# Hybrid decoder step: RWKV's eight low-rank steps grouped into the first lot of pages, its other steps from the seventh piece on, and TensorE turning the identity into unused banks in front of five waits

## Chip, cores and metric

One core of one Trainium2 chip runs the whole program. The metric is the device time of one execution in microseconds, as the median of several runs. "PE" is TensorE, "ACT" ScalarE, "DVE" VectorE, "POOL" GpSimd and "SP" SyncE, which only issues transfers here.

## What is computed

The reference is one step of a one-layer decoder. All tokens (512 prompt tokens, 16 meta tokens, 8 sequences with 8 new tokens each) are RMS-normalised and go through one input projection. Half of the projected features feed forgetting attention (8 heads of 64), the other half RWKV-7 time mixing (8 heads of 64). Both results are concatenated and go through an output projection, a SwiGLU FFN and a last RMSNorm. Cut to what matters here:

```python
xn = rms_norm(x, ln1_g);  proj = x_ext @ w_in
# forgetting attention; the new tokens of sequences read 32 pages of 128 past keys and values per sequence
attn = softmax(q k^T / 8 + c_q - c_k) v
# RWKV-7: low-rank steps, then keys' norm, then a recurrence over tokens
w_log = -softplus(-(w0 + tanh(wl) @ w2)) - 0.5;  decay = exp(-exp(w_log))
a = sigmoid(a0 + al @ a2);  g = sigmoid(gl) @ g2
kk = (k * k_k) / max(norm(k * k_k), 1e-12);  k = k * (1 + (a - 1) * k_a)
S = S * decay + (S @ -kk) (kk * a)^T + v k^T;  y = S @ r
out = (group_norm(y) + sum(r * k * r_k) * v) * g
h = x + concat(attn, out) @ w_out;  y = rms_norm(h + ffn(rms_norm(h)))
```

## The kernel before

**Prologue.** For each of five row tiles of x, ACT squares it, DVE scales it (L1902), PE turns it with eight transposes (L741) and DVE copies the turned tile out of PSUM (L1913, `take_rows`). Then eight more transposes (L782) and the input projection follow (L800, 16 instructions for half an item of 301 columns).

**Prompt part.** Projection items, the values' rows (L773) and the prompt's attention in 32 steps share PE until about 324 us.

**Lots.** The past of the eight sequences is read in pairs of sequences, four pages at a time: 4 pairs of 8 lots, 32 lots in all. SP loads each page of keys or values, for both sequences of the pair, into a ring of four slots, and a slot is loaded again once PE has read it. On each engine a generator `all_lots` emits a lot in eight pieces. In a lot `turn_keys` (L1241) turns a page of keys of two sequences in eight transposes, ACT copies it (`take_keys`, L1788, two copies), and `page_scores` (L1255) multiplies it with the queries; `turn_probs` (L1281) turns the previous lot's probabilities, and `lot_values` (L1300) weighs its values. At the end of a lot DVE's `add_scores` (L2288, L2291, L2295) reads the scores, and ACT's `exp_lot` (L1798) exponentiates them in the next lot, ahead of that lot's second pair of key copies. PE turns into two banks in turn, so a second turn after one must wait for the copy of the one before the last.

**RWKV between the pieces.** A second generator `rwkv_rest` holds RWKV's steps, the same number on PE, ACT and DVE. After each piece, every engine runs steps until `rwkv_due(piece)` of them are done; a list `COSTS` gives each step's share. Each engine executes its instructions strictly in the order so written. `rwkv_pre` is the preparation, 17 steps: `row_sums_of` (PE L911), eight `low_rank(j)` (PE L931, two products of 320 columns; ACT's Sigmoid L1661), ACT's Sqrt (L1668) and DVE's reciprocal (L2072) of the key norm, four `spread_norm` (PE L917, DVE L2056), DVE's scans (L2076), and three Exp over 2560 columns (ACT L1683, L1684, L1687). Counted from piece 0, `low_rank(0)` stands behind piece 5, `low_rank(1)` to `(7)` behind pieces 8 to 21, the three Exp behind pieces 24 and 26 (lot 3), and the tiles of the recurrence begin behind piece 46. In the recurrence's last tile, `sample_states`, DVE masks two heads at a time (L2231) and PE multiplies them with keys (L1170), one group g per step; step g=0 stands in piece 5 of lot 23 and step g=1 in its piece 7.

ACT holds one set of function tables; each change of set shows as ACT_TABLE_LOAD. The Sigmoids, the Sqrt and the lots' Exp need three sets. Behind the lots stand the output projection and the FFN, which keep PE full from 905 us to the end.

The lines that set the order are

```python
COSTS = N_PRE * [4] + (12 + 18 * (NTILE - 1)) * [2] + (23 + 16) * [3]
def rwkv_due(piece):
    budget = sum(COSTS) * (piece + 1) // (8 * LOTS - 20)
    return sum(c <= budget for c in itertools.accumulate(COSTS))
rest, done = rwkv_rest(), 0
for piece, _ in enumerate(all_lots()):
    while done < rwkv_due(piece):
        next(rest)
        done += 1
```

## Time and profile before

| | |
|---|---|
| median of 3 runs | 1407.38 us (1405.04 to 1408.07) |
| profiled execution, its time | 1404.47 us |
| profiled execution, its span | 1402.7 us |
| PE busy | 1309.2 us, 93% of the span |
| DVE, ACT, POOL busy | 567.0, 387.1, 110.6 us |
| mean granted clock of PE | 0.985 |
| HBM traffic | 203.06 MB read, 14.41 MB written |

The span leaves out 1.8 us of the execution's time. The profiled execution lies 2.9 us under the median. The page says where engines are busy; a list by stretch shows busy time, granted clock (1.00 is 2.4 GHz, 0.50 is 1.2 GHz) and the DMA engines' share; the list of waits names who released an idle engine; the timeline gives single instructions.

### The profile page before, as it was taken

How to read it: one execution, taken by the hardware profiler on the slowest of the kernel's cores; microseconds unless marked ns; L12 is line 12 of the kernel's file. 1: busy time of each engine (PE TensorE's matmuls, PEld its weight loads, DVE VectorE, ACT ScalarE, POOL GpSimd, SP SyncE). 2: the span in 40 equal slices, each digit the busy share in tenths (PEclk: the TensorE clock that was granted, in tenths of full speed). 3: DMA queues.
4: the chain of work that ended last, by engine and by line, in shares of the span. 5: the costliest groups of instructions: out<-in, count | busy, mean ns of one | idle time of the engine just before them, and what ended most of it. 6: DMA issues, size and time to landing. Idle time of an engine off the chain costs nothing.

```text
span 1402.7 us, 28552 instructions
## 1 busy us (share of the span) xinstructions
PE 1309.2 (93%) x11707; PEld 953.8 (68%) x11707; DVE 567.0 (40%) x1084; ACT 387.1 (28%) x769; POOL 110.6 (8%) x219
## 2 busy tenths in 40 slices
PE   5999999997889999999998789999999999999997
PEld 4764666665567677777774555457777777778886
DVE  5012355554573443443426233255334333372322
ACT  3010333235654444435452453210000000000001
POOL 6273200000000000000300101000000000000000
PEclk9999999998999999999999999999999999999999
DMA  6167310006688777778886988901123113123101
GB/s 221 61 140 181 111 61 10 29 0 229 231 308 300 231 230 268 228 255 273 255 275 203 366 309 285 306 7 60 61 61 119 61 60 101 42 83 124 42 8 61
DMA packets 128844, 219.37 MB, mean 156 GB/s; under 512 B 11484, under 2 KB 46375, under 8 KB 128711
## 3 DMA queue, kind: packets, MB, share of 16 engines
q1 hardware_dynamic: 120818, 193.64, 41.4%
q0 software_dynamic: 7824, 23.85, 6.2%
q8 instruction: 93, 1.52, 0.5%
q14 instruction: 41, 0.33, 0.1%
q10 hardware_dynamic: 68, 0.02, 0.0%
HBM read 203.06 MB, written 14.41 MB: 155 GB/s over the span
## 4 chain that ended last, share of the span: by engine, by line
PE 86%; DVE 6%; ACT 3%; issue 2%; DMA 2%; SPq 0%; POOL 0%; POOLq 0%; DVEq 0%; ACTq 0%
PE PS L1435 21%; PE PS L800 13%; PE PS L1517 9%; PE PS L1241 7%; PE PS L1255 4%; PE PS L1367 4%; PE PS L1300 4%; PE PS L773 2%; DMA out_wkv_prompt<-arena 1%; PE PS L1526 1%; PE PS L1055 1%; PE PS L1059 1%; PE PS L1065 1%; PE PS L882 1%; PE PS L1281 1%
## 5 line engine op out<-in xcount | busy, mean ns | idle before, releaser
L1435 PE MATMUL PS<-arena 128*128 128x288 f32 x1232 | 300.3, 405 | 1.1 <-issue 0.6
L1435 PEld LDWEIGHTS PS<-arena 128*128 128x128 f32 x1232 | 232.2, 189 | 68.1 <-DVE arena L2525 1.0
L800 PE MATMUL PS<-arena 128*128 128x301 f32 (+1 forms) x736 | 195.9, 423 | 0.0
L1788 ACT ACTIVATE arena<-PS 128x512 f32<-128x512 f32 x256 | 140.9, 595 | 166.7 <-PE PS L1241 166.7
L800 PEld LDWEIGHTS PS<-arena 128*128 128x128 f32 (+1 forms) x736 | 135.5, 187 | 53.9 <-issue 12.3
L1241 PE MATMUL PS<-arena 128*128 128x128 f32 x1024 | 145.5, 283 | 20.1 <-ACT arena L1788 7.1
L1241 PEld LDWEIGHTS PS<-arena 128*128 128x128 f32 x1024 | 115.2, 144 | 47.9 <-issue 25.9
L1517 PE MATMUL PS<-arena 128*128 128x256 f32 x616 | 134.4, 379 | 0.0
L1517 PEld LDWEIGHTS PS<-arena 128*128 128x128 f32 x616 | 116.2, 189 | 17.7 <-issue 0.8
L1255 PE MATMUL PS<-arena 128*32 128x128 f32 x2048 | 83.6, 280 | 0.1
L1300 PE MATMUL PS<-arena 128*32 128x256 f32 x1024 | 68.7, 385 | 2.6 <-DMA arena<-in_cache_v 1.9
L1255 PEld LDWEIGHTS PS<-arena 128*32 128x32 f32 x2048 | 51.0, 110 | 24.0 <-issue 17.3
L1367 PE MATMUL PS<-arena 128*128 128x512 f32 x128 | 59.1, 602 | 0.0
L2140 DVE TENSOR_TENSOR arena<-PS,arena 128x512 f32<-128x512 f32 (+2 forms) x56 | 36.0, 660 | 48.6 <-PE PS L1055 35.9
L2325 DVE SCALAR_TENSOR_TENSOR arena<-arena,PS 128x256 f32<-128x256 f32 x32 | 15.4, 480 | 82.3 <-PE PS L1300 82.1
L2578 DVE TENSOR_TENSOR arena<-PS,arena 128x256 f32<-128x256 f32 x36 | 14.4, 422 | 80.9 <-PE PS L1517 80.9
L1300 PEld LDWEIGHTS PS<-arena 128*32 128x32 f32 x1024 | 28.3, 109 | 27.7 <-issue 12.5
L1599 ACT ACTIVATE arena<-PS 128x602 f32<-128x602 f32 (+1 forms) x23 | 15.5, 673 | 105.3 <-PE PS L800 105.3
L1367 PEld LDWEIGHTS PS<-arena 128*128 128x128 f32 x128 | 22.8, 189 | 26.5 <-issue 26.5
L651 POOL DMA_DIRECT2D forgets_after<-arena x64 | 36.9, 601 | 47.3 <-DVE arena L1958 32.8
L2508 DVE TENSOR_TENSOR arena<-PS,arena 128x288 f32<-128x288 f32 x22 | 10.1, 458 | 73.5 <-PE PS L1435 73.5
L414 POOL DMA_DIRECT2D out_y_sample<-arena x2 | 1.1, 537 | 483.4 <-DVE arena L2621 483.4
(383 smaller groups left out, 1510.4 us busy)
## 6 DMA issues: line engine op xcount, KB each, us to landing
arena<-in_cache_k SPq DMA_DIRECT2D x256, 256.0 KB, 4.2
arena<-in_cache_v SPq DMA_DIRECT2D x256, 256.0 KB, 4.4
arena<-in_w_gate SPq DMA_DIRECT2D x11, 1024.0 KB, 5.5
arena<-in_w_up SPq DMA_DIRECT2D x11, 1024.0 KB, 8.1
arena<-in_w_down SPq DMA_DIRECT2D x8, 1408.0 KB, 6.4
arena<-in_w_in SPq DMA_DIRECT2D x5, 2048.0 KB, 11.7
forgets_after<-arena POOLq DMA_DIRECT2D x64, 128.0 KB, 8.5
arena<-forgets_after SPq DMA_DIRECT2D x32, 256.0 KB, 5.1
```

The lines of the kernel that those rows point to most:

```text
L651: pool.dma_start(forgets_after[b, DS * h:DS * h + DS].rearrange("t (c k) -> c t k", k=PAGE), src)\
L773: ins = mm(o, xnT[:, k, 17 + P * (i - 1):17 + P * i], w, start=(k == 0), stop=(k == KT - 1))
L800: ins = mm(PS[0:width, bank, 0:HALF], wring[:, c % 2, k, c0:c0 + width], xnT[:, k, half * HALF:(half + 1) * HALF], start=(k == 0), stop=(k ...
L1241: ins = tr(PS[:, bank, g * P:(g + 1) * P], Kr[:, i, q, g * P:(g + 1) * P], ident)
L1255: ins = mm(PS[ROWS[2 * q + gp], SCORE, i * P:(i + 1) * P], QB[:, 2 * (L // NLOT) + q, g, :], KTs[:, (2 * i + q) % LOT, g, :], start=(gg == ...
L1300: ins = mm(PS[ROWS[r], OUT, 0:QW], PTs[:, i, ROWS[r]], Vr[:, i, r // 2, QW * (r % 2):QW * (r % 2) + QW], start=(i == 0), stop=(i == LOT - ...
L1367: ins = mm(PS[rows, E + 2 * (n % 2) + half, :], mixT[:, k, cols], wo[:, k, half * NB:(half + 1) * NB], start=(k == 0), stop=(k == KT - 1), ...
L1435: ins = mm(PS[:, bank, 0:HO], weights[:, j], moving[:, j], start=(first and j == 0), stop=(j == KH - 1), skip_group_check=not first)
L1517: ins = mm(PS[:, bank, 0:QC], weights[:, j, q * P:(q + 1) * P], moving[:, j], start=(first and j == 0), stop=(j == NR - 1), skip_group_che ...
L1599: av(dst.rearrange("p (a b) -> p a b", a=2), src, ACT.Copy, scale=scale).then_inc(S["proj_taken"], 1)
L1788: av(KTs[:, (2 * i + q) % LOT], PS[:, T_USE[("k", L, i, q)] % 2, :].rearrange("p (g n) -> p g n", g=NG), ACT.Copy)\
L2140: return tt(dst, src, mask.unsqueeze(1).unsqueeze(1).to_broadcast([n_p, a, b, n]), ALU.mult)
```

## The change

`keep_busy(n, bank)` lets PE turn the identity n times into a bank that nothing reads. It is called in six lines, around five waits or rows of waits: 24 turns before the parameters are waited for; 16, 8, 7 and 9 after the turns of row tiles 1 to 4; 12 on either side of `new_scores(0)`; 30 ahead of the first group of `sample_states`; 12 ahead of the spread of the last norm. They are 130 turns in all.

The first step of `rwkv_rest` (now `row_sums_of` and `low_rank(0)`) runs before the first piece, and the other low-rank steps stand behind pieces 0, 1 and 2: two, two and three of them. In the last of these ACT also takes the gate's Sigmoid, which stood before the lots, and the Sqrt. Nothing more of RWKV runs until piece 9; from there the steps follow at nearly the old rate. `spread_norm` gets four steps of its own, the three Exp are cut into halves, one half per step, and DVE's scans move to the second piece's step, ahead of the reciprocal. The tiles of the recurrence come in the same piece or one piece earlier than before. The new tokens' Exp (`exp_new(0)`) moves from before the lots to piece 3, its turn and copy to piece 6.

```diff
         SMP = NTILE
-        N_PRE = 17
+        N_PRE = 18
 
...
         HALVES = [slice(0, 64), slice(64, P)]
-        COSTS = N_PRE * [4] + (12 + 18 * (NTILE - 1)) * [2] + (23 + 16) * [3]
+        N_AHEAD = 4
+        COSTS = N_AHEAD * [0] + (N_PRE - N_AHEAD) * [4] + (12 + 18 * (NTILE - 1)) * [2] + (23 + 16) * [3]
         N_RWKV = len(COSTS)
...
                 if L % NLOT == 0:
-                    if i == 2 and L < LOTS:
+                    if i == (2 if L else 3) and L < LOTS:
                         use_t(("n", L // NLOT), "prn_taken", L // NLOT + 1)
...
         def rwkv_due(piece):
-            budget = sum(COSTS) * (piece + 1) // (8 * LOTS - 20)
+            if piece + 2 < N_AHEAD:
+                return piece + 2
+            budget = sum(COSTS) * max(0, piece - 6) // (8 * LOTS - 27)
             return sum(c <= budget for c in itertools.accumulate(COSTS))
...
+
+            def keep_busy(n, bank):
+                for _ in range(n):
+                    tr(PS[:, bank, 0:P], ident, ident)
+
+            keep_busy(24, 6)
             pe.wait_ge(S["par_in"], 16 * (len(PAR_ROWS) + 2))
...
                 ins.then_inc(S["xT_turned"], 1)
+                keep_busy((0, 16, 8, 7, 9)[i], 6)
             pe.wait_ge(S["xnT_ready"], NTILE)
...
                 pe.wait_ge(S["consts"], 4)
-                pe.wait_ge(S["lr_act"], 2)
-                g, bank = j % 4, E + 2 * (j % 2 if j < 4 else 1)
+                pe.wait_ge(S["lr_act"], 1)
+                g, bank = j % 4, E + 2 * (j % 2)
                 if j == 1:
                     pe.wait_ge(S["root_in"], 1)
                 elif j:
-                    pe.wait_ge(S["lr_taken"], j - 1 if j < 4 else j)
+                    pe.wait_ge(S["lr_taken"], j - 1)
                 w = slice(g * P, (g + 1) * P)
...
                 if n == 0:
-                    pe.wait_ge(S["lr_taken"], 3)
+                    pe.wait_ge(S["lr_taken"], 7)
                 else:
...
             def rwkv_pre():
-                yield
+                low_rank(0)
                 row_sums_of(T2, 1, E + 2)
-                low_rank(0)
                 yield
...
                 low_rank(3)
-                spread_norm(0)
-                yield
-                for n in range(3):
-                    low_rank(4 + n)
-                    spread_norm(n + 1)
-                    yield
+                low_rank(4)
+                yield
+                low_rank(5)
+                low_rank(6)
                 low_rank(7)
                 yield
-                for _ in range(6):
+                for n in range(NG):
+                    spread_norm(n)
+                    yield
+                for _ in range(7):
                     yield
...
                 yield
+                keep_busy(30, E + 2)
                 for g in range(NG):
...
                 pe.wait_ge(S["g2_in"], 16)
+                pe.wait_ge(S["lr_act"], 2)
                 for g in range(NG):
...
                 yield
+                keep_busy(12, E + 2)
                 pe.wait_ge(S["hs_in"], 6)
...
                         lot_values(L - 1, 0)
-                    if j == 0:
+                    if j == 0 and L:
                         turn_new(pr)
...
                         lot_values(L - 1, 1)
+                    else:
+                        turn_new(0)
                     yield
...
             ins.then_inc(S["rn_turned"], 1)
+            keep_busy(12, OUT)
             new_scores(0)
+            keep_busy(12, OUT)
             def rows_of(i):
...
 
-            rest, done = rwkv_rest(), 0
+            rest, done = rwkv_rest(), 1
+            next(rest)
             for piece, _ in enumerate(all_lots()):
...
             av(XR[0:64, 12, :], XR[0:64, 12, :], ACT.Tanh).then_inc(S["lr_act"], 1)
-            av(XR[:, 13, :], XR[:, 13, :], ACT.Sigmoid).then_inc(S["lr_act"], 1)
-
...
                 act.wait_ge(S["lr_ready"], j + 1)
-                bank = E + 2 * (j % 2 if j < 4 else 1)
+                bank = E + 2 * (j % 2)
                 src = PS[:, bank:bank + 2, 0:TL // 2]
...
             def rwkv_pre():
-                yield
                 low_rank(0)
                 yield
+                low_rank(1)
+                low_rank(2)
+                yield
+                low_rank(3)
+                low_rank(4)
+                yield
+                low_rank(5)
+                low_rank(6)
+                low_rank(7)
+                av(XR[:, 13, :], XR[:, 13, :], ACT.Sigmoid).then_inc(S["lr_act"], 1)
                 act.wait_ge(S["root_in"], 1)
                 av(Rn, Rn, ACT.Sqrt).then_inc(S["root_done"], 1)
-                low_rank(1)
-                low_rank(2)
-                yield
-                low_rank(3)
-                yield
-                low_rank(4)
-                yield
-                low_rank(5)
-                yield
-                low_rank(6)
-                yield
-                low_rank(7)
+                yield
                 yield
                 act.wait_ge(S["L_ready"], 1)
-                av(AR[:, 1], Kd, ACT.Exp, scale=-E_HALF).then_inc(S["decays"], 1)
-                av(AR[:, 0], AR[:, 0], ACT.Exp, scale=-E_HALF).then_inc(S["decays"], 1)
-                yield
-                act.wait_ge(S["decays"], 1)
-                av(Kd, Kd, ACT.Exp, scale=E_HALF).then_inc(S["decays"], 1)
-                yield
+                for n, (dst, src, scale) in enumerate(((AR[:, 1], Kd, -E_HALF), (AR[:, 0], AR[:, 0], -E_HALF), (Kd, Kd, E_HALF))):
+                    if n == 2:
+                        act.wait_ge(S["decays"], 2)
+                    for half in (slice(0, 2), slice(2, 4)):
+                        av(dst[:, half], src[:, half], ACT.Exp, scale=scale).then_inc(S["decays"], 1)
+                        yield
                 for _ in range(7):
...
                     take_keys(L, 2)
+                    if L == 0:
+                        exp_new(0)
                     yield
...
             av(RNT, PS[:, SCORE, :].rearrange("p (r n) -> p r n", r=NPAIR)[:, :, 64:P], ACT.Copy).then_inc(S["rn_taken"], 1)
-            exp_new(0)
-            rest, done = rwkv_rest(), 0
+            rest, done = rwkv_rest(), 1
+            next(rest)
             for piece, _ in enumerate(all_lots()):
...
                 yield
+                for g in range(NG):
+                    dve.wait_ge(S["lr_taken"], g + 1)
+                    ch(v.tensor_tensor_scan(Kd[:, g], chunk_mask, AR[:, 0, g], 0.0, ALU.mult, ALU.add))
+                yield
                 dve.wait_ge(S["root_done"], 1)
                 v.reciprocal(Rn, Rn).then_inc(S["hs_in"], 1)
                 yield
-                dve.wait_ge(S["lr_taken"], 4)
-                for g in range(NG):
-                    ch(v.tensor_tensor_scan(Kd[:, g], chunk_mask, AR[:, 0, g], 0.0, ALU.mult, ALU.add))
                 norm_keys(0)
-                yield
-                norm_keys(1)
                 ch.wait()
                 tt(AR[:, 0], Kd, AR[:, 0], ALU.subtract).then_inc(S["L_ready"], 1)
                 yield
-                norm_keys(2)
-                yield
-                norm_keys(3)
-                yield
+                for n in range(1, NG):
+                    norm_keys(n)
+                    yield
                 dve.wait_ge(S["hs_taken"], 4)
...
                 yield
-                dve.wait_ge(S["decays"], 3)
                 ch(tt(Bd, Bd, kk, ALU.mult))
                 yield
+                dve.wait_ge(S["decays"], 4)
                 ch(stt(AR[:, 0], kk, -1.0, AR[:, 0], ALU.mult, ALU.mult))
...
                 ch.wait()
+                dve.wait_ge(S["decays"], 6)
                 ch(tt(Bd, Bd, Kd, ALU.mult))
...
                     yield
-                    if j == 0:
+                    if j == 0 and L:
                         take_new_probs(pr)
                     yield
                     yield
+                    if L == 0:
+                        take_new_probs(0)
                     if L:
...
 
+            rest, done = rwkv_rest(), 1
+            next(rest)
             dve.wait_ge(S["rn_taken"], 1)
             add_new(0)
-            rest, done = rwkv_rest(), 0
             for piece, _ in enumerate(all_lots()):
```

## Rows read from the trace of the kernel before

**Rows 1.** The page, part 1: engines' busy time over the whole span.

```profile
PE 1309.2 (93%) x11707; PEld 953.8 (68%) x11707; DVE 567.0 (40%) x1084; ACT 387.1 (28%) x769; POOL 110.6 (8%) x219
```

**Rows 2.** Lots 1, 3, 4: length; PE, PEld, DVE, ACT, POOL; clock; DMA share, GB/s.

```profile
343.00:368.00 25.00, 19.91 (x170) 14.07 (x171) 15.94 (x15) 15.90 (x23) 0.00 (x0) 0.86 0.69 236
382.50:397.80 15.30, 9.46 (x124) 6.76 (x122) 11.10 (x13) 12.38 (x13) 0.00 (x0) 0.78 0.68 232
397.80:408.60 10.80, 9.15 (x135) 6.46 (x136) 10.66 (x14) 5.65 (x11) 0.00 (x0) 1.00 1.01 360
```

**Rows 3.** By stretch, PE alone: the stretches at the lower clock.

```profile
271.40:278.20 6.80, 6.26 (x18) 0.50 0.01 2
326.00:336.20 10.20, 6.30 (x52) 0.50 0.95 319
349.90:356.70 6.80, 4.43 (x11) 0.50 0.28 103
387.40:394.30 6.90, 4.64 (x40) 0.51 0.34 118
749.20:756.10 6.90, 6.05 (x19) 0.51 0.01 4
```

**Rows 4.** Timeline of the prologue; in brackets idle time and releaser.

```profile
8.73 0.33 PE L735 MATMUL PS<-arena 58*128 58x58 f32 x1 [8.73 <-DMA ptab<-in_page_table]
...
16.42 1.97 PE L741 MATMUL PS<-arena 128*128 128x128 f32 x8 [2.39 <-DVE arena L1902]
...
22.31 1.27 DVE L1913 TENSOR_TENSOR arena<-PS,arena 128x512 f32<-128x512 f32 x2
22.44 1.97 PE L741 MATMUL PS<-arena 128*128 128x128 f32 x8 [1.03 <-DVE arena L1902]
24.45 1.29 DVE L1913 TENSOR_TENSOR arena<-PS,arena 128x512 f32<-128x512 f32 x2 [0.87 <-PE PS L741]
25.79 1.88 PE L782 MATMUL PS<-arena 128*9 128x128 f32 x8 [1.38 <-DVE arena L1913]
27.47 2.72 PE L800 MATMUL PS<-arena 128*128 128x301 f32 x7
```

**Rows 5.** Timeline, PE, start of the lots.

```profile
326.85 0.66 PE L1268 MATMUL PS<-arena 128*32 128x64 f32 x16 [2.29 <-ACT arena L1829]
330.53 3.97 PE L1241 MATMUL PS<-arena 128*128 128x128 f32 x16 [3.02 <-DMA arena<-in_cache_k]
341.75 0.65 PE L1255 MATMUL PS<-arena 128*32 128x128 f32 x16
```

**Rows 6.** Waits of PE from 323.9 to 410 us: total, times, longest.

```profile
PE PS L1281 <- ACT arena L1788: 11.5, 3, 5.8
```

**Rows 7.** Groups of ACT by line, 323.5 to 392 us: busy us, mean ns.

```profile
L1661 ACT ACTIVATE arena<-PS,arena 128x640 f32<-128x640 f32 x8 | 6.2, 794 | 4.1 <-PE PS L931 4.1
L1661 ACT ACT_TABLE_LOAD x4 | 5.1, 1283 | 0.1
L1683 ACT ACTIVATE arena<-arena 128x2560 f32<-128x2560 f32 x1 | 2.3, 2337 | 0.0
```

**Rows 8.** Groups of DVE by line, 323.5 to 424 us.

```profile
L2072 DVE RECIPROCAL arena<-arena 128x640 f32<-128x640 f32 x1 | 4.2, 4153 | 2.4 <-ACT arena L1668 2.4
```

**Rows 9.** Chain that ended last: start, us; eight key turns, two low-rank products.

```profile
365.62 1.03 PE PS L1241 x8
366.64 1.10 PE PS L931 x4
```

**Rows 10.** Timeline around `sample_states`, PE, then DVE.

```profile
740.77 1.93 PE L1170 MATMUL PS<-arena 64*64 64x512 f32 x8
750.05 3.67 PE L1170 MATMUL PS<-arena 64*64 64x512 f32 x8 [4.66 <-DVE arena L2231]
...
747.50 2.50 DVE L2231 TENSOR_TENSOR arena<-arena 64x512 f32<-64x512 f32 x4
```

**Rows 11.** Timeline, PE, the last norm's spread.

```profile
828.65 1.35 PE L917 MATMUL PS<-arena 128*128 128x320 f32 x4 [1.97 <-DVE arena L2265]
```

More of the change, by code:

```diff
@@ L1663, in rwkv_pre @@
             def rwkv_pre():
-                yield
                 low_rank(0)
                 yield
-                act.wait_ge(S["root_in"], 1)
-                av(Rn, Rn, ACT.Sqrt).then_inc(S["root_done"], 1)
                 low_rank(1)
```

2 lines of the change are left out of this document (added).

## Prediction

> **What bounds the kernel.** I began with the page's busy times: PE is busy 1309.2 us of a span of 1402.7, everything else under half of it [rows 1]. So a change pays only if it removes idle time of PE, time at the lower clock, or work, and here 130 turns are added. Next I listed busy time and granted clock by stretch. Each stretch at the lower clock follows idle time on PE, and in it the same work takes twice as long: 16 key turns took 3.97 us at 330.5 us, and 8 took 1.03 us at 365.6 us [rows 5, 9]. The five stretches in the lots, the attention and the recurrence cost half their busy time: 3.1, 3.2, 2.2, 2.3 and 3.0 us [rows 3]. The records show no clock for the first 29 us, but 8 turns take 1.97 us there, which is the lower clock's time [rows 4]. Then I went through the first lots, which the change rewrites. Lot 1 takes 25.0 us, of which PE is busy 19.9; lot 3 takes 15.3 with 9.5 busy; lot 4 takes 10.8 with 9.15 busy and a DMA share of 1.01 [rows 2]. So in lots 1 and 3 PE waits for somebody, and in lot 4 the transfers are the limit. The list of waits names one: L1281, `turn_probs`, waited three times, 11.5 us in all, the longest 5.8 [rows 6]. Its releaser is written as the key copies, but these stand in ACT's order behind table loads, low-rank Sigmoids and, in lot 3, two whole Exp of 2.3 us each: it is ACT's order that PE waits for.
>
> **Prologue.** 24 turns at the lower clock are 24 x 1.97/8 = 5.9 us; PE sat idle there until 8.7 us [rows 4], so they cost nothing and may raise the clock. The turns after row tiles 1 to 4 lie in idle time of 1.0 to 2.4 us a tile [rows 4]: at full clock (1.03/8 = 0.13 us [rows 9]) 16 take 2.1 us and 7 to 9 take 0.9 to 1.2 us. DVE sets the pace of the tiles, so nothing is won before the last. Behind it, if the clock is full: DVE's last copy starts at 23.6 (end of the one before) and not at 24.45, which is 0.85 us; L782 takes 1.0 and not 1.88 us; and the first seven of L800 take about 1.9 and not 2.72 us [rows 4]. The sum is 2.5 us, and it goes through whole, since PE has no idle time in the next 100 us. With gaps left between the bursts the clock may fall again before the last tile, and then 16 turns at the lower clock (3.9 us in a gap of 2.4) delay the chain a little. I take -2.0, with bounds +1.5 and -2.6.
>
> **Start of the lots.** Before, PE waited 2.29 us for ACT and 3.02 us for the first keys [rows 5]. The keys land at 330.5 whatever PE does. Up to then PE now has 12 turns (1.6 us), the new scores (0.5), 12 turns (1.6), `low_rank(0)` (1.1) and the row sums (1.3), from 324.6: it ends with the row sums near 330.4, since these wait for DVE's squares until 328.9. So the 24 turns cost nothing. They hold the clock, and the stretch from 326.0 to 336.2 no longer costs its 3.2 us (part of which was hidden under arriving keys: I count 2.5).
>
> **Low-rank steps in lot 0.** A low-rank step is two products, four instructions, and 1.10 us at full clock [rows 9], and ACT takes 0.8 us for each [rows 7], so PE and ACT alternate without a stall. From 330.5 PE has seven steps (7.7 us), three pages of keys (3.3) and two page scores (1.3): it is through at 342.7. ACT then still has the last Sigmoid (0.8), the gate's Sigmoid (0.8), a table load (1.3 [rows 7]), the Sqrt (0.8), and only then the copies of the third page. The fourth page's turn needs the bank of the third: PE waits from 342.7 to about 345. Another table load and `exp_new(0)` (1.8 us) stand ahead of the fourth page's copies, which holds PE another 1.3 and 0.5 us. DVE's reciprocal (4.2 us [rows 8]) follows the Sqrt and ends at 348.6, just as `new_values` would ask for the copy queued behind it. Lot 0 so ends near 349.5, 6.5 us later than before, with 7.7 us of low-rank work done ahead. These waits add up to 4.3 us, and busy time is so thin from 342.7 to 348 that I expect the clock to fall once: +2.5 us, as the other falls cost.
>
> **Lots 1 to 4.** Before, ACT loaded tables ten times from the gate's Sigmoid to the first long Exp, four of them ahead of low-rank Sigmoids at 1.28 us each [rows 7]; now three loads do, and the seven saved are 9.0 us of ACT's time. The waits of L1281 go, 11.5 us, and two stretches of lower clock with them, 2.2 and 2.3 us. The halved Exp put 1.2 us in front of a copy where 4.7 or more stood. Then the limit of lot 4 takes over. A lot moves 16 pages of 128 x 512 floats and a bias of the same size, 4.46 MB. At the 360 GB/s of a full DMA that is 12.4 us, while lot 4 took 10.8, since its first pages lay in the rings already [rows 2]. I take 11.8, between the two. PE alone needs 9.15 us [rows 2]. So my walk is: lot 0 ends at 349.5; lot 1 has three spreads, 9.2 + 3 x 1.2 + 1 for small waits = 13.7, and 2.5 for the clock: 365.7; three lots at 11.8: 401.1. Before, the same point, with the same RWKV steps done but for one pair of sums, stood at 408.6. I take -7.5. Without the transfers' limit lots 2 to 4 would take 3 x 9.6 = 28.8 us, which is 6.6 better; with new waits as long as a whole Exp on DVE's side (its steps are 2.8 us each, and three a lot and the lots' own work nearly fill DVE) it could be -2. These are the bounds: -2 and -14.
>
> **Thirty turns before the first group of new states.** They stand ahead of the step g=0. There PE arrived at 740.7 and waited 0.3 us; the long wait of 4.66 us is that of g=1 [rows 10]. Behind g=0 PE weighs values and scores pages, DVE adds the scores, ACT exponentiates, DVE takes the new scores, and only then comes the masking (2.50 us at 747.5) that g=1 waits for. That whole chain hangs on PE's work after the 30 turns, so it moves by them: 30 x 0.13 = 3.9, less 0.3. The wait of 4.66 us stays, and the fall of the clock in it too. +3.5; bounds 0 (if the chain had slack that I don't see) and +4.1.
>
> **The rest.** Twelve turns (1.6 us) before the last norm's spread lie in a wait of 1.97 us [rows 11]: 0. From piece 45 on the steps come in the same piece or one earlier, so order and waits are those of before: 0.
>
> **Sum.** -2.0 - 7.5 + 3.5 = -6.0 us against the profiled execution, 1404.5, gives 1398.5. That execution is 2.9 us under the median; -6.0 from 1407.4 gives 1401.4. I forecast **1401**.
>
> **Does turning hold the clock?** The trace says so: at the lower clock from 326.0, PE was idle or turned keys for most of the time (16 turns from 330.5 on, 3.97 us), and at 336.2 the clock rose [rows 3, 5]. By that the turns count as work. The Trainium skill (TensorE: Matmul & The Clock Gate, Part 4: PE-mode transpose) says the contrary, that transposes don't count as busy in the same way and full clock doesn't engage for them; by it the sum would lose the clock terms, and the time would be that of the third rival below. The trace disagrees with it here.
>
> **Rivals.** (1) *The transfers don't bind and the clock holds.* For it: DMA had a share of only 0.68 and 0.69 in lots 1 and 3 [rows 2], so the rings might be full when the fast lots come, and a lot took 10.8 us, not 11.8. Three lots at 10.8 are 3 us better, no fall in lot 0 another 2.5, the prologue 0.5: -12, 1395.5. Chance 0.20. (2) *Given back.* The waits in lot 0 grow (ACT's copies of page 3 behind Sqrt, DVE's reciprocal ahead of the new tokens' probabilities), the clock falls twice, and lots 2 to 4 run at the transfers' pace anyway: lots -3, prologue -1, thirty turns +3.5: 1407, no change. Chance 0.15. (3) *Turns don't hold the clock*, the one that ends slower. Then the turns after tiles 1 to 4 take 3.9, 2.0, 1.7 and 2.2 us at 0.246 each, longer than the gaps, and by following the tiles L800 starts 4.2 us late; the 24 around the new scores take 5.9 us and make the first key turn 3.3 us late; the lots' waits still go but their clock terms don't: -7.5 + 3.3 + 2.5; the thirty cost 3.5. With the prologue's 4.2 instead of -2.0 the sum is +6.0: 1413. It decides from the point where a burst of turns ends after its wait does, some 10 turns a gap. Against it stands the rise at 336.2. Chance 0.08. The forecast itself has 0.57.
>
> **Range and chances.** What a measurement of this kernel can tell from no change is 0.2%, 2.8 us: faster means under 1404.6, slower over 1410.2. The forecast's own range is 1396 to 1406, the clock's falls alone being worth 2 to 3 us each and not tied to the program where they come by chance. With the first two rivals inside I give 1394 to 1408. Faster: 0.50 of the first case, all of rival 1, a little of rival 2: 0.72. Slower: rival 3 and the edge of rival 2: 0.09. Same: 0.19.
>
> **What the profile after would show.** L782 at 1.0 us and L800 starting near 25.9: the prologue's step is right; turns of 0.25 us there: wrong. `add_scores` of lots 0 and 4 near 347 and 399 (both 2 us earlier than in the walk, for the prologue): right; lots 2 to 4 with a DMA share near 1.0 show the transfers as the limit. L1281's waits on ACT under 3 us in all; one lower-clock stretch between 320 and 400 and not three. A wait of about 4.7 us before L1170's second group and none filled before the first: the thirty turns are cost. If the wait before g=1 has shrunk instead, that step is wrong. The forecast fails most easily if lots 2 to 4 are faster than 11.8 us or if a new wait of DVE's stands before `exp_lot`.

## The result and the profile after

The changed kernel takes **1388.64 us** (median of 4 runs, 1388.36 to 1392.19) against 1406.41 for the kernel before, a ratio of 0.9875 with a 95% interval of 0.9856 to 0.9894: 17.8 us faster. Forecast were 1401 and a range of 1394 to 1408. The direction was right and the size was a third of what came; the time lies below the range.

The page of the changed kernel, part 1, answers to [rows 1]:

```profile
span 1386.2 us, 28803 instructions
PE 1315.2 (95%) x11837; PEld 962.3 (69%) x11837; DVE 566.6 (41%) x1084; ACT 376.4 (27%) x765; POOL 111.0 (8%) x219
```

PE does 130 instructions more and is busy 6.0 us more, and the span is 16.5 us shorter: idle time went. ACT lost 10.7 us of work, which is mostly table loads.

The stretches of the changed kernel between the `add_scores` of lots 0 to 4, as in [rows 2] (PE, PEld, DVE, ACT, POOL; clock; DMA share, GB/s):

```profile
344.30:356.40 12.10, 11.51 (x149) 8.10 (x142) 7.00 (x11) 7.96 (x13) 0.00 (x0) 1.00 0.95 330
356.40:367.90 11.50, 10.91 (x141) 7.87 (x142) 5.75 (x13) 9.01 (x14) 0.00 (x0) 1.00 0.96 328
367.90:378.90 11.00, 9.44 (x138) 6.97 (x139) 10.86 (x14) 6.71 (x13) 0.00 (x0) 1.00 1.03 376
378.90:389.60 10.70, 8.93 (x130) 6.07 (x129) 10.56 (x13) 5.64 (x11) 0.00 (x0) 1.00 1.05 386
```

Lots 1 to 4 took 66.1 us together and now take 45.4. The DMA share is 0.95 or more in each, where it was 0.69 and 0.68 in lots 1 and 3. It doesn't follow that the transfers set the length of a lot. In lots 1 and 2 PE is busy all but 0.6 us. In lots 3 and 4 it is DVE: busy 10.86 of 11.0 and 10.56 of 10.7 us, and in its timeline nothing stands idle from one `add_scores` (L2302) to the next. The last operations of lot 3:

```profile
375.73 2.82 DVE L2113 TENSOR_TENSOR arena<-arena 128x2560 f32<-128x2560 f32 x1
378.47 0.48 DVE L2339 SCALAR_TENSOR_TENSOR arena<-arena,PS 128x256 f32<-128x256 f32 x1
378.86 0.69 DVE L2302 TENSOR_TENSOR arena<-PS,arena 128x512 f32<-128x512 f32 x1
```

PE ends the page scores at 378.04, 0.8 us before DVE comes to them. The chain of work that ended last names, from 367.9 to 395.0 us, DVE alone and "issue", time in which an engine waits for nothing that the profile shows; no transfer and no other engine stands in it. Its longest pieces on DVE there:

```profile
369.43 2.82 DVE arena L2106
373.35 2.47 DVE arena L2110 x3
375.82 1.89 DVE arena L2113
380.38 2.82 DVE arena L2116
386.50 2.22 DVE arena L2125
391.14 2.82 DVE arena L2128
```

The kernel before had the same limit in its lot 4: DVE is busy 10.66 of 10.8 us there [rows 2], and from 397.8 us to the next `add_scores` at 408.6 its chain too names DVE and "issue" alone. The waits of PE in the changed kernel from 345 to 395 us, where [rows 6] had 11.5 us on one line:

```profile
PE PS L1254 <- ACT arena L1806: 1.6, 4, 0.9
PE PS L1254 <- ACT arena L1801: 1.4, 4, 0.3
PE PS L1254 <- DMA arena<-in_cache_k: 0.7, 2, 0.6
PE PS L1313 <- DMA arena<-in_cache_v: 0.6, 1, 0.6
PE PS L1294 <- ACT arena L1801: 0.4, 1, 0.4
```

The turn of probabilities (now L1294) waits 0.4 us. The prologue of the changed kernel on PE, which answers to [rows 4] (L740 are the turns of the identity, L750 those of the row tiles, L792 and L810 what follows):

```profile
2.75 4.32 PE L740 MATMUL PS<-arena 128*128 128x128 f32 x24 [2.75 <-POOL arena L577]
...
13.67 3.09 PE L740 MATMUL PS<-arena 128*128 128x128 f32 x16
16.60 1.04 PE L750 MATMUL PS<-arena 128*128 128x128 f32 x8
...
24.86 1.05 PE L792 MATMUL PS<-arena 128*9 128x128 f32 x8 [0.40 <-DVE arena L1928]
25.75 1.94 PE L810 MATMUL PS<-arena 128*128 128x301 f32 x7
```

L792 takes 1.05 instead of 1.88 us, L810 starts at 25.75 instead of 27.47, and its first seven take 1.94 instead of 2.72. The first group of new states, answering to [rows 10], PE and then DVE:

```profile
718.53 3.50 PE L740 MATMUL PS<-arena 128*128 128x128 f32 x30
721.95 1.94 PE L1181 MATMUL PS<-arena 64*64 64x512 f32 x8
731.24 3.68 PE L1181 MATMUL PS<-arena 64*64 64x512 f32 x8 [4.66 <-DVE arena L2245]
...
728.67 2.51 DVE L2245 TENSOR_TENSOR arena<-arena 64x512 f32<-64x512 f32 x4
```

The thirty turns stand in front of the first group, and the second group's wait is 4.66 us, to the hundredth what it was.

All kernels were then laid beside each other by the same marks: the start of the first projection item, the turn of the new tokens' mask that opens the lots, and the `add_scores` of lots 0, 4, 22 and 24. Executions differ by a few us, in part by where the clock falls, so the parts say more than the totals. (us; the last column is the length of the stretch at the lower clock near 270 us, in the prompt's attention.)

| kernel | first item | mask turned | to lot 0 | lots 1-4 | lots 5-22 | 23-24 | near 270 |
|---|---|---|---|---|---|---|---|
| before | 27.5 | 323.9 | 18.6 | 66.1 | 317.7 | 43.7 | 6.8 |
| changed | 25.8 | 318.5 | 25.8 | 45.4 | 314.5 | 48.0 | none |
| changed, again | 25.1 | 320.9 | 25.9 | 46.7 | 314.9 | 47.6 | 6.8 |
| order only | 27.3 | 324.1 | 26.7 | 45.8 | 319.8 | 43.7 | 6.8 |
| turns only | 24.8 | 319.2 | 18.3 | 66.1 | 319.1 | 47.9 | 3.4 |
| no thirty | 24.7 | 317.4 | 26.1 | 45.4 | 317.0 | 44.9 | none |
| thirty later | 25.1 | 317.7 | 25.9 | 45.4 | 316.7 | 41.4 | none |
| no prologue turns | 26.7 | 322.1 | 25.8 | 45.6 | 318.7 | 47.2 | 3.4 |
| the same, again | 26.4 | 323.1 | 25.8 | 46.7 | 318.2 | 47.6 | 6.8 |
| no scores turns | 24.6 | 317.3 | 25.4 | 45.9 | 317.7 | 47.9 | none |
| lots loaded | 25.9 | 321.6 | 25.9 | 48.7 | 319.6 | 47.5 | 6.8 |
| whole Exp | 25.9 | 318.6 | 25.7 | 48.0 | 319.1 | 47.9 | none |
| halves in before | 27.4 | 323.9 | 18.8 | 65.3 | 318.0 | 43.7 | 6.8 |
| tables back | 24.9 | 319.3 | 26.5 | 53.7 | 315.4 | 47.0 | 3.4 |
| best1 | 25.9 | 320.2 | 25.7 | 45.6 | 315.7 | 41.4 | 3.4 |
| no start 24 | 25.8 | 318.5 | 25.6 | 45.4 | 318.2 | 47.7 | none |
| no tile turns | 27.4 | 323.1 | 25.6 | 45.4 | 315.9 | 47.2 | 3.4 |
| best2 | 25.8 | 320.1 | 25.7 | 45.5 | 315.9 | 41.4 | 3.4 |

By these marks the 16.5 us of the profiled executions are: up to the mask -5.5, lot 0 +7.2 (the low-rank steps done there), lots 1 to 4 -20.7, lots 5 to 22 -3.2, lots 23 and 24 +4.3, behind them +1.4.

### The profile page after: what moved, and what is told of

The parts are those of the page before. It is cut to its first block, busy times and chain, and to the rows that moved or that the text cites. A ratio compares the mean times of both kernels' runs of the same rounds, so it can differ in the third digit from the quotient of the medians.

```text
span 1386.2 us, 28803 instructions
## 1 busy us (share of the span) xinstructions
PE 1315.2 (95%) x11837; PEld 962.3 (69%) x11837; DVE 566.6 (41%) x1084; ACT 376.4 (27%) x765; POOL 111.0 (8%) x219
## 4 chain that ended last, share of the span: by engine, by line
PE 86%; DVE 6%; ACT 3%; issue 2%; DMA 2%; SPq 0%; POOL 0%; POOLq 0%; DVEq 0%; ACTq 0%
PE PS L1453 22%; PE PS L810 13%; PE PS L1535 9%; PE PS L1254 7%; PE PS L1268 4%; PE PS L1384 4%; PE PS L1313 4%; PE PS L783 2%; DMA out_wkv_prompt<-arena 1%; PE PS L1544 1%; PE PS L1075 1%; PE PS L1065 1%; PE PS L1069 1%; PE PS L892 1%; PE PS L927 1%
## 5 line engine op out<-in xcount | busy, mean ns | idle before, releaser
L810 PE MATMUL PS<-arena 128*128 128x301 f32 (+1 forms) x736 | 193.0, 418 | 0.0
L810 PEld LDWEIGHTS PS<-arena 128*128 128x128 f32 (+1 forms) x736 | 133.6, 185 | 52.6 <-issue 10.2
L2154 DVE TENSOR_TENSOR arena<-PS,arena 128x512 f32<-128x512 f32 (+2 forms) x56 | 35.9, 658 | 47.2 <-PE PS L1065 32.8
L1313 PEld LDWEIGHTS PS<-arena 128*32 128x32 f32 x1024 | 28.0, 108 | 26.9 <-issue 10.8
L1384 PEld LDWEIGHTS PS<-arena 128*128 128x128 f32 x128 | 22.8, 189 | 26.5 <-issue 26.5
## 6 DMA issues: line engine op xcount, KB each, us to landing
arena<-in_w_in SPq DMA_DIRECT2D x5, 2048.0 KB, 11.7
```

Source lines behind the costliest of these rows:

```text
L810: ins = mm(PS[0:width, bank, 0:HALF], wring[:, c % 2, k, c0:c0 + width], xnT[:, k, half * HALF:(half + 1) * HALF], start=(k == 0), stop=(k ...
L1313: ins = mm(PS[ROWS[r], OUT, 0:QW], PTs[:, i, ROWS[r]], Vr[:, i, r // 2, QW * (r % 2):QW * (r % 2) + QW], start=(i == 0), stop=(i == LOT - ...
L1384: ins = mm(PS[rows, E + 2 * (n % 2) + half, :], mixT[:, k, cols], wo[:, k, half * NB:(half + 1) * NB], start=(k == 0), stop=(k == KT - 1), ...
L2154: return tt(dst, src, mask.unsqueeze(1).unsqueeze(1).to_broadcast([n_p, a, b, n]), ALU.mult)
```

## Experiments

**The order without the turns, and the turns without the order.** `order_only` takes all six calls of `keep_busy` out of the changed kernel; `turns_only` puts them into the kernel before.

```diff
-            keep_busy(24, 6)
...
-                keep_busy((0, 16, 8, 7, 9)[i], 6)
...
-                keep_busy(30, E + 2)
...
-                keep_busy(12, E + 2)
...
-            keep_busy(12, OUT)
             new_scores(0)
-            keep_busy(12, OUT)
```

> The changed kernel without any of the 130 turns of the identity; the order of the steps is the new one. Theory (the order gives most of the gain, by freeing ACT in lots 0 to 3; the turns give only the clock at two places and cost the thirty): against the changed kernel it loses 2.5 us in the prologue and 2.5 to 3 us of lower clock behind 330 us, and wins 3.3 us by the missing thirty: 1389 to 1392. Lots 0 to 4 take what they take in the changed kernel within 3 us. Rival (the turns hold the clock all through lots 0 to 4 and this is most of the gain): 1396 or more, with two or three stretches of lower clock between 320 and 400 us.

> The kernel before with the same 130 turns at the same places, steps in the old order. Theory (order gives most): prologue -2.5, the stretch of lower clock after 326 us gone, -2.5, the thirty turns +3.3: 1404 to 1406, and the wait of 5.8 us before the turn of probabilities in lot 3 is still there. Rival (the turns are the gain): under 1398.

Measured: order only 1394.18 us (ratio 0.9914, 0.9895 to 0.9933), turns only 1405.07 (0.9994, 0.9977 to 1.001). The time of the first is 2 us above what the theory gave and under the rival's, though two stretches of lower clock came, as the rival had it (3.4 us each, from 329.7 and 346.8); that of the second is the theory's. From the mask's turn to the scores of lot 4 the order alone takes 72.5 us and the changed kernel 71.2, where the kernel before takes 84.7 and the turns alone leave 84.4. So the whole gain of the lots is the order's. Up to the mask it is the other way: the turns alone gain and the order can't.

**The thirty turns.** `no_thirty` takes them out, `thirty_later` has them ahead of the second group, in that group's own bank:

```diff
-                keep_busy(30, E + 2)
                 for g in range(NG):
+                    if g == 1:
+                        keep_busy(30, E + 3)
                     pe.wait_ge(S["um_ready"], 2 * g + 2)
```

> The changed kernel without the thirty turns ahead of the first group of new states. Theory of the prediction (they delay the chain that the second group's wait hangs on, at full price less 0.3 us): 3.3 to 3.6 us faster than the changed kernel, 1385.2, the wait of 4.7 us before the second group unchanged. Rival (they hold the clock or lie in a wait): the same time within 1 us, or slower, with a longer stretch of lower clock behind them.

> The changed kernel with the thirty turns ahead of the second group instead of the first, into that group's own bank. Theory: the wait of 4.7 us becomes 0.8 us of wait and 3.9 us of turns, the chain isn't delayed, and the clock doesn't fall behind it, which cost about 3 us: 1382 to 1383.5, 5 to 6.5 us faster than the changed kernel. Rival (the fall of the clock there has another cause): the time of the kernel without the thirty.

Measured: 1386.32 us (ratio 0.9858, 0.9840 to 0.9876) without, 1384.62 (0.9845, 0.9829 to 0.9861) later. In lots 23 and 24 the four kernels stand at 48.0 (first group), 44.9 and 43.7 (none; two kernels) and 41.4 us (second group). Ahead of the first group the turns cost 3.1 to 4.3 us, moved one step they win 2.3 to 3.5. The two kernels with none differ in the clock too: it fell for 10.2 us in `no_thirty` and for 6.8 in `order_only`. The timeline of PE in `thirty_later`:

```profile
724.79 3.50 PE L740 MATMUL PS<-arena 128*128 128x128 f32 x30
729.52 1.93 PE L1182 MATMUL PS<-arena 64*64 64x512 f32 x8 [1.23 <-DVE arena L2246]
```

The wait is 1.23 us of what was 4.66, and the second group takes 1.93 instead of 3.68 us, since the clock no longer fell. The theory gave 5 to 6.5 us; the totals give 4.0 and, against the second measurement of the changed kernel, 6.8, and the part gives 6.6.

**The prologue's turns.** `no_prologue_turns` and `no_prologue_again` are one kernel, without the 24 and without those after the tiles; `no_start_24` and `no_tile_turns` lack one of the two calls each.

> The changed kernel without the 24 turns at the start and those after the row tiles; all others stay. Theory (the prologue's turns bring the full clock to its last row tile, and nothing later depends on them): the first projection item starts 1.7 to 2.8 us later and its first instructions run at the lower clock; 3 us slower than the changed kernel in all, 1391.6. Rival (they also keep the clock in the prompt's attention 270 us in, where the kernel before and the one without any turns each show a stretch at the lower clock and three of four kernels with them show none): that stretch comes back, 3 us more, 1394 to 1395.

> The kernel without the prologue's turns once more. By the profiles the turns are worth 3.0 us up to the turn of the mask, once the stretches of lower clock near 270 us are taken out; its median was 6 to 9 us above the changed kernel's two. Theory (3 us and chance): 1391 to 1395. Rival (they are worth 6 us or more by something later): 1396 to 1398 again.

> The changed kernel without the 24 turns at the start, with those after the row tiles. Theory (the 16 turns after the second tile raise the clock by themselves, since in the changed kernel it had fallen again by then): the first projection item starts as early as with them, within 0.5 us; the time of the changed kernel. Rival (a cold start of the 16 delays the tiles, or the clock rises too late): 1 to 3 us slower.

> The changed kernel with the 24 turns at the start and none after the row tiles. Theory (the clock falls in the tiles' gaps, and the last tile is turned at the lower clock): as slow as the kernel without both, the first item starting 1.7 to 2.8 us later. Rival (the 24 turns are enough): the time of the changed kernel.

Measured: 1397.62 and 1398.32 us without both (ratios 0.9950 and 0.9949, 0.9932 to 0.9969 and 0.9932 to 0.9966), 1393.74 without the 24 (0.9891 to 0.9937), 1394.81 without the tiles' (0.9901 to 0.9935). Which call counts shows in the timelines of PE. First `no_tile_turns`:

```profile
22.37 1.97 PE L750 MATMUL PS<-arena 128*128 128x128 f32 x8 [1.03 <-DVE arena L1916]
25.72 1.88 PE L791 MATMUL PS<-arena 128*9 128x128 f32 x8 [1.38 <-DVE arena L1927]
```

Then `no_start_24`:

```profile
24.92 1.05 PE L791 MATMUL PS<-arena 128*9 128x128 f32 x8 [0.40 <-DVE arena L1927]
```

Without the tiles' turns the last tile and L791 run at the lower clock as in the kernel before; without the 24 nothing is lost up to the first item, to 0.1 us. So the 24 do nothing there: the clock they raise falls again before the row tiles. The tile turns bring the first item 1.7 us forward and shorten its first seven instructions by 0.8: 2.5 us. Up to the mask it is 2.5 to 3 us: the six kernels with them and without a fall near 270 us stand at 317.3 to 318.6, and the four without them and with a fall of 6.8 us at 323.1 to 324.1, of which 3.1 us is the fall's. The medians lie further off: 6 to 10 us from the changed kernel's two without both calls, 3 to 6 without the tiles' turns, and 2 to 5 without the 24. Some of this is the fall near 270: it came in all six profiled executions without the tile turns and in six of twelve with them. The rest of the distance isn't explained by any stretch that the profiles show, and stays open.

**The turns around the new scores.**

> The changed kernel without the 12 and 12 turns around the new tokens' first scores. Theory (with the new order PE has low-rank work before the first keys, so the clock is nearly safe there; without any turns the stretch from the turn of the new tokens' mask to the scores of lot 4 took 72.5 us and with them 71.2 to 71.5): 1 to 1.5 us slower, 1389.5 to 1390. Rival (they are what saves the clock at the start of the lots): a stretch of 6.8 us or more at the lower clock there and 3 us lost, 1391.5 or more.

Measured: 1390.88 us (0.9890, 0.9872 to 0.9909), between the theory's and the rival's. The parts say nothing is lost: 25.4 us to lot 0 and 45.9 in lots 1 to 4, and no fall at 326. The order gives PE low-rank work while it waits for the first keys, and that is enough for the clock here and in `best2` below. It wasn't in `order_only`, where these turns are missing too: there the clock fell for 3.4 us at 329.7, and lot 0 ended 26.7 us after the mask. What the 24 turns save is nothing in two executions and may be up to 1 us in the third.

**What limits lots 2 to 4.** `lots_loaded` gives PE eight turns more in six steps that are empty on PE:

```diff
-                for _ in range(7):
+                for n in range(7):
+                    if n < 6:
+                        pe.wait_ge(S["lr_taken"], 8)
+                        keep_busy(8, E + 2)
                     yield
```

> The changed kernel with eight more turns of the identity, 1.03 us of PE, in each of six steps of lots 2 to 4 in which PE has nothing of RWKV to do. Theory A (transfers limit lots 2 to 4, as the prediction had it): lots 2 to 4 keep their 11.5, 11.0 and 10.8 us within 0.5 us each, and the time stays within 1.5 us of the changed kernel's. Theory B (PE and its waits for ACT limit them, the rings' reserve covers the transfers): the 6.2 us show in full, 1394.5 to 1395. In between: the share that shows is PE's.

Measured: 1395.65 us (0.9934, 0.9916 to 0.9952). From the scores of lot 1 to those of lot 4 it takes 35.4 us against 33.3, to those of lot 5 52.0 against 49.5. The stretches of `lots_loaded` for lots 2 to 4:

```profile
360.80:373.20 12.40, 11.81 (x149) 8.78 (x150) 5.77 (x13) 9.01 (x14) 0.00 (x0) 1.00 1.00 352
373.20:385.20 12.00, 11.40 (x158) 9.12 (x159) 11.03 (x14) 6.66 (x12) 0.00 (x0) 1.00 1.03 362
385.20:396.20 11.00, 10.41 (x149) 8.12 (x149) 10.72 (x13) 5.54 (x11) 0.00 (x0) 1.00 1.03 374
```

Of 6.2 us added, 2.1 to 2.5 show. Lot 2 has one of the six bursts and gets longer by 0.9 us, all of it: PE is the limit there. Lot 3 has three, 3.3 us, and gets longer by 1.0. Lot 4 has two, 2.2 us, and gets longer by 0.2 to 0.3. So in lots 3 and 4 something else than PE sets the pace, but theory A has the wrong name for it. DVE stays busy 11.03 us in lot 3 and 10.72 of the 11.0 in lot 4; in lot 3 it now waits 0.83 us for PE, in lot 4 for nobody. PE's waits for transfers, 1.3 us in these two lots of the changed kernel, are gone here, and lot 4 isn't shorter for it. No run lightened DVE, so this limit is read from the traces and not from an experiment on DVE alone. The total is 4 to 7 us higher than the changed kernel's two. The profiled execution, the slowest of six, has falls of the clock near 270, 344 and 535 us; the changed kernel's second execution has the first two of them, its first none of this length. What the median's distance consists of isn't shown.

**Whole Exp in the changed kernel, halves in the kernel before.**

```diff
-                    for half in (slice(0, 2), slice(2, 4)):
-                        av(dst[:, half], src[:, half], ACT.Exp, scale=scale).then_inc(S["decays"], 1)
-                        yield
+                av(AR[:, 1], Kd, ACT.Exp, scale=-E_HALF).then_inc(S["decays"], 1)
+                av(AR[:, 0], AR[:, 0], ACT.Exp, scale=-E_HALF).then_inc(S["decays"], 1)
+                yield
```

> The changed kernel with the three Exp whole, as before: two of 2.3 us in one step, the third in the next, and no halves. Theory (whole Exp stand in ACT's order ahead of the key copies and were the wait of 5.8 us in lot 3): PE waits 3 to 5 us once between the scores of lots 0 and 3, and the clock may fall behind it, 2 us: 3 to 6 us slower, 1392 to 1395. Rival (the moved low-rank steps, not the halves, made the gain; ACT has time in lots 1 to 3 now that no tables are loaded): less than 1.5 us.

> The kernel before with nothing changed but the three long Exp of 2560 columns: the first two cut into halves that stand one to a step, the third into halves that stand together in the next step. Theory (whole Exp in ACT's order were the wait of 5.8 us of the turn of probabilities in lot 3, and the clock fell behind it): that wait shrinks to under 2 us, the lower clock near 387 us goes, 4 to 7 us faster than before. Rival (the wait goes to another place, because a table load and DVE's long operations stand there too): under 2 us faster.

Measured: whole Exp 1395.27 us (0.9929, 0.9909 to 0.9950), of which 2.6 us lie in lots 1 to 4; a wait of PE of this size appears in lot 1:

```profile
PE PS L1268 <- ACT arena L1801: 2.4, 1, 2.4
```

Halves in the kernel before: 1403.59 us (0.9976, 0.9961 to 0.9992), but only 0.8 us of it in lots 1 to 4. Lot 3 took 11.6 instead of 15.3 us, and lot 4 13.7 instead of 10.8: the waits of `halves_in_before` from 343 to 424 us show a turn of probabilities still waiting, five times and 10.2 us in all, 4.7 of them in lot 1, where low-rank Sigmoids and table loads are where they were.

```profile
PE PS L1281 <- ACT arena L1789: 10.2, 5, 4.7
```

Lot 4 has no low-rank step. What it lost it lost on DVE, which waited 2.85 us for halves of the third Exp (L1687) and was busy all the rest of the lot:

```profile
397.17 2.83 DVE L2104 SCALAR_TENSOR_TENSOR arena<-arena 128x2560 f32<-128x2560 f32 x1 [1.23 <-ACT arena L1687]
402.15 2.83 DVE L2111 TENSOR_TENSOR arena<-arena 128x2560 f32<-128x2560 f32 x1 [1.62 <-ACT arena L1687]
```

So the halves are worth 2.6 us in the new order and almost nothing in the old. The theory was right about the wait of lot 3; the rival was right that the time goes to another place, DVE's long operations in lot 4.

**Table loads put back.** `tables_back` has a Sigmoid of one column ahead of the second half of each Exp:

```diff
                     for half in (slice(0, 2), slice(2, 4)):
+                        if half.start:
+                            av(small[:, 4:5], small[:, 4:5], ACT.Sigmoid)
```

> The changed kernel with a Sigmoid of one column, on data that nobody reads, ahead of the second half of each of the three Exp, so that ACT loads two tables (2.56 us) in each of three steps of lots 1 to 3. Theory (table loads in ACT's order among the lots were the other half of what PE waited for): 3 to 6 us slower than the changed kernel from the turn of the mask to the scores of lot 4. Rival (ACT has room in these lots, and the transfers set the pace anyway): under 1 us there.

Measured: 1398.83 us (0.9944, 0.9923 to 0.9966). Lots 1 to 4 take 53.7 us instead of 45.4 and 46.7. The groups of ACT in `tables_back` from 345 to 395 us:

```profile
L1701 ACT ACT_TABLE_LOAD x3 | 3.8, 1283 | 0.1
L1702 ACT ACT_TABLE_LOAD x3 | 3.8, 1283 | 0.0
```

7.7 us of table loads on an engine that is busy 7.3 of 11.3 us a lot cost 7.0 to 8.3 us, more than the theory gave. They don't cost it evenly: lot 1 is as long as before (12.1 us), lot 2 is 3.1 us longer, lot 3 5.2 and lot 4 not at all. Two stretches of lower clock came with them (3.4 and 6.8 us from 372.6 and 379.5, PE busy 3.40 and 5.18 us in them); at half clock that is up to 4.3 us of the sum, nearly all in lot 3. So the waits behind the loads and the clock that fell in them have about equal parts. This is the experiment that says what the old order cost.

**Two better versions.** `best1` is `thirty_later` with 14 turns in lot 0's wait for the Sqrt; `best2` is `thirty_later` without the 36 turns around the new scores and before the last norm's spread.

```diff
+                    if L == 0:
+                        pe.wait_ge(S["lr_taken"], 7)
+                        keep_busy(14, E)
                     turn_keys(L, 3)
```

> The changed kernel with the thirty turns ahead of the second group of new states (as in the kernel that had them there) and 14 more turns in lot 0, ahead of the fourth key page's turn, where PE waited 2.7 us for ACT behind the Sqrt and the clock fell for 3.4 us. Theory: against the kernel with the thirty moved alone 1 to 1.7 us from the start of the lots to the scores of lot 1, no lower clock near 340 us; 1383. Rival (the turns only move the fall by a few us, since ACT's next table load leaves another gap): no difference.

> The changed kernel with the thirty turns ahead of the second group and without the 12 and 12 around the new scores and the 12 before the last norm's spread. Theory (these 36 lie in waits and hold nothing that counts): the time of the kernel that has them, 1384.4 within 1.5 us. Rival (they save a fall of the clock each, 1.5 to 3 us): 1386 or more.

Measured: 1384.22 us (0.9837, 0.9816 to 0.9858) and **1383.14 us** (0.9844, 0.9824 to 0.9864). They and `thirty_later` can't be told apart. In `best1` the fall near 340 us is gone, lot 0 ends 25.7 us after the mask instead of 25.9, and lots 1 to 4 take the same 45.6 us: a clock that falls for 3.4 us there costs nothing. In its place stands a wait of 1.08 us for key copies that ACT has behind a table load and `exp_new(0)`:

```profile
344.74 0.41 PE L1289 MATMUL PS<-arena 128*64 128x128 f32 x2 [1.08 <-ACT arena L1805]
```

A fall of 6.8 us, in the changed kernel's second execution, cost 1.3 us of lot 1. The 36 turns of `best2` do nothing that shows in its time.

**The changed kernel again.**

> The changed kernel once more, unaltered, beside the others of this batch: how far its 1388.6 us, its absent stretch of lower clock in the prompt's attention and its short lots 5 to 22 (314.5 us between two scores where seven other kernels took 316.7 to 319.8) were chance. Theory (they were lucky): 1389 to 1392, with lots 5 to 22 at 316 to 320 us. Rival (they belong to the kernel): 1388.5 within 1 us and 314 to 315 us again.

Measured: 1391.44 us (0.9877, 0.9855 to 0.9900), so the ratio to the kernel before is what it was, and the total is the theory's; lots 5 to 22 are the rival's. The fall near 270 us came, and the mask is turned 2.4 us later; lots 5 to 22 took 314.9 us again. The three kernels with the old order took 317.7 to 319.1 us there, the fifteen with the new one 314.5 to 319.8; the five with a fall of the clock in it stand at 318.2 or more, the ten without at 314.5 to 318.2. If anything of the gain lies there it is 1 to 2 us.

## Why the prediction was wrong

**Reading of the bound: right for lots 1 and 3, wrong for lot 4.** PE's idle time behind ACT in lots 1 and 3 was the place of the gain, and `tables_back` confirms that table loads among the lots are paid in full, waits and clock together. In lot 4 the prediction named the transfers, by their share of 1.01; the limit was DVE's order, busy 10.66 of 10.8 us in the same row. And the chain of the kernel before goes in lot 1 not only through three table loads but also through DVE's scans (L2076, 5.64 us from 356.4), which the change moved as well; no run moves them alone, so their part of the gain in lot 1 stays open.

**Lots 1 to 4, -7.5: the step that failed.** "Then the limit of lot 4 takes over" was priced as the transfers' pace, 11.8 us a lot, and lot 1 at 16.2 us. From the mask to lot 4 the change gave -13.5 us (-12.1 in the second execution). The removals that the prediction listed come to 16 us (11.5 of waits, 4.5 of clock) and the new waits in lot 0 to 4.3; the difference, 11.7, was close. The walk then took back more than was due. It let lot 0 end 25.6 us after the mask, and it took 25.8. It gave lot 1 13.7 us with three spreads and 2.5 for a fall of the clock: the third spread stands behind lot 1's scores, the fall came in lot 0 and lasted 3.4 us, and lot 1 took 12.1 (13.4 where a fall of 6.8 us reached into it). And it gave lots 2 to 4 11.8 us each as the transfers' pace, 35.4; they took 33.3. That makes 4.1 and 2.1 us of the 6.0, with 0.2 the other way in lot 0. The second term is wrong in its mechanism and not only in its size: lot 2's 11.5 us are PE's, and the 11.0 and 10.8 us of lots 3 and 4 are DVE's order, back to back. DMA moved 376 and 386 GB/s in these two lots, above the 360 from which I had worked out 12.4 us, and the slots still held enough that PE waited for transfers only 1.3 us in both together, none of it on the chain. That 11.8 came within 1 us of each lot is luck.

**Lot 0: right.** PE was to wait from 342.7 to 345 behind the gate's Sigmoid and the Sqrt. In the changed kernel, 5.5 us earlier:

```profile
335.77 1.04 PE L1254 MATMUL PS<-arena 128*128 128x128 f32 x8
340.07 1.70 PE L1254 MATMUL PS<-arena 128*128 128x128 f32 x8 [2.68 <-ACT arena L1801]
```

A wait of 2.68 us, and the clock fell once behind it, for 3.4 us. `best1` showed that the fall cost nothing; I had counted 2.5 us.

**Prologue, -2.0: right, and 0.5 us short.** The first item started 1.7 us earlier and its first seven instructions took 0.8 us less, 2.5 us, which is the sum that the prediction worked out before it took 2.0; up to the mask the kernels give 2.5 to 3 us. The 24 turns that I let "may raise the clock" did raise it, and it fell again before the first tile; the tile turns did the work.

**What was not in the sum.** A fall near 270 us cost the profiled execution of before 3.1 us, which the changed kernel's profiled execution didn't have. The prediction named such falls as chance and left them out of the sum. It came in twelve of the eighteen profiled executions, more often without the tile turns; the cause isn't settled. Lots 5 to 22, for which the prediction had 0, took 3.2 us less in the profiled execution; 1 to 2 of them may be the change's.

**The start of the lots: right in time, the reason only in part.** The clock held there, but `no_scores_turns` and `best2` show that it holds without the 24 turns too; in `order_only` it fell for 3.4 us instead of 10.2.

**Thirty turns, +3.5: right.** 3.1 to 4.3 us were measured, the wait of 4.66 us stayed where it was, and the clock fell in it. That it fell for 10.2 us instead of 6.8 isn't the turns' doing: in `no_thirty` it was 10.2 as well. **The last norm's twelve, 0: right**; the row behind them, answering to [rows 11], waits 0.51 us instead of 1.97:

```profile
810.15 1.53 PE L740 MATMUL PS<-arena 128*128 128x128 f32 x12
812.19 1.35 PE L927 MATMUL PS<-arena 128*128 128x320 f32 x4 [0.51 <-DVE arena L2279]
```

**Does turning hold the clock?** Yes. In the changed kernel the low stretch ended at 16.1 us, after 28 instructions that are all turns, 16 of tiles and 12 of the identity (length, busy us of PE, clock, DMA share, GB/s):

```profile
9.25:16.10 6.85, 5.90 (x28) 0.50 0.98 319
16.10:25.70 9.60, 7.18 (x62) 1.00 1.04 394
```

The second stretch too has only turns in it, 62 of them, and stays at full clock. The rule of the Trainium skill (TensorE: Matmul & The Clock Gate, Part 4: PE-mode transpose), that full clock doesn't engage for transposes, doesn't hold here: 1.00 was granted through those 62.

**The rivals.** The first (-12, 1395.5) was nearest, and still 7 us short. Its premise, that the transfers don't bind, is what the traces show for lots 1 to 4; but it took 10.8 us for lot 2 as well, which PE holds at 11.5, and it kept the high price of lot 1, 13.7 us. The second, that the waits in lot 0 give the gain back, is closed by the 71.2 us from the mask to lot 4 against 84.7. The third needed turns that don't raise the clock.

**The range: too narrow below.** The lots' own bound was -14 and the runs came to -13.5, while the low end of 1394 left some 13 us for all terms together. With 2.5 us of prologue and 3.2 of lots 5 to 22, less 4.3 for lots 23 and 24 and 1.4 behind them, the parts make -13.5, about what the second execution shows (1402.7 to 1389.3 us of span). From the median of 1407.4 that just reaches the low end; the fall near 270 us that didn't come, 3.1 us, takes the first execution below it.

## What to carry to other kernels

A table load in an in-order engine that feeds the critical one costs more than its share of busy time says: 7.7 us of them cost 7 to 8 us, the clock that fell in the waits included, although ACT was idle a third of the time. So group steps by their table set, and do it where the critical engine has other work. Fill a wait with turns only after finding whose wait it is: thirty turns one step too early cost 3 us or more, and one step later won 2 to 3. And before a sum names the next limit, look at every engine in the stretch and at the chain: a DMA share of 1.01 stood beside a DVE that was busy 10.66 of 10.8 us, and it was DVE that held the lots.

## What was not expected of the hardware

- Thirty turns of 128x128 back to back take 3.50 us at full clock, 0.117 us each; eight between other work take 1.03 to 1.09 us, 0.13 each.
- 24 turns raised the clock at 5.8 us, and at 9.25 us, in the second of two idle times of 1.6 and 1.3 us, it was lower again. With the tile turns it stayed full from 16.1 us on through gaps of 0.9 and 1.2 us.
- A fall of the clock of 3.4 us in lot 0, near 340 us, costs nothing: `best1`, which doesn't have it, takes 45.6 us for lots 1 to 4 against 45.4. A fall of 6.8 us that reaches into lot 1 cost 1.3 us.
